# The first six weight units: VectorE sums the squares, GpSimd splits three units, and loads and products change order

## The chip, the cores and the metric

The kernel is one program on one core of a Trainium2 chip. The metric is the device time of one execution in microseconds (us). The engines are TensorE (PE, with its weight loads shown as PEld), VectorE (DVE), ScalarE (ACT), GpSimd (POOL) and the queue that issues most transfers, SyncE (SP).

## The reference

One sequence of 512 tokens, 1024 features wide, goes through two blocks. The first is RWKV-7 and mLSTM mixing with a mixture of experts, the second a convolution and a state-space mixer with a dense feed-forward. What matters here is how the first block begins:

```
mod = silu(c) @ ada_w + ada_b                 # 6 x 1024 values
sh_m, sc_m, ... = split(mod, 6)
h = x * rsqrt(mean(x * x) + EPS) * mix_norm_w * (1.0 + sc_m) + sh_m
proj = h @ w_in                               # float32, 1024 x 3336
```

## The kernel before

**Data.** Features lie on the 128 partitions, so `x` is a tile `xT` of KD = 8 pieces of 128 x 512. A weight unit is 128 x 1024 float32: eight 128 x 128 tiles that give one output tile of 128 x 512. Every float32 product is made of three passes on fp32r halves. The upper half of a weight unit is a copy with rounding (`act_upper`, on ScalarE), the lower half is the unit less that copy. The activations are split likewise: `in_h_hi` is written by ScalarE, and `dve_lower` writes the rest `h_lo` into `hT_r`. A product is upper weight x `hi`, lower weight x `hi`, upper weight x `lo`.

**The first FIRST = 6 units** have a buffer of their own (`first_w`, `first_hi_r`, `first_lo_r`) and are worked side by side by `first_units`: for each of the eight pieces k, twelve products with `hi` for the six outputs, then six with `lo`. The later units (6 and on) go through a ring of six slots, one after the other, with GpSimd making their lower halves (`pool_lower`).

**The order by engine** is written by hand, with semaphores. `S(name)` is a semaphore, and `GOES_ON` lets a name count on where another has ended.

- SP loads `c`, `x` in two halves, two modulation rows, the columns, the six units, then modulation rows 2 to 15. From row 4 on each waits until a slot of `mod_ring` (four slots) was used.
- ScalarE squares the eight pieces of `xT` into `hT`, makes the upper halves of units 0 to 2, takes the logarithm and the exponential of the sum (`act_std`: the reciprocal root), makes the upper half of unit 3, and goes into `act_shift_split`, which writes `in_h_hi` piece by piece and makes the upper halves of units 4 and 5 after piece 0.
- TensorE sums the squares over partitions with a matrix of ones (`norm_sum`: eight float32 products of two matmuls each), then does `first_units`.
- VectorE multiplies modulation rows with silu(c) and sums them (`modulate`, two rows give shift and scale of one piece), makes the gain (`early_gain`), subtracts for the lower halves (`first_lower`), and for each piece does the scaling `hT = xT * gain * rstd`, two modulation rows of a later piece, `dve_lower` and the gain. Units 3 to 5 are subtracted after piece 0's scaling, ahead of its `dve_lower`.
- GpSimd has three memsets, then waits for unit 6.

Of the kernel before, what the change touches and what calls it, by code (L numbers as in the profile page):

```python
# [11 lines left out]
ALU = mybir.AluOpType  # L12
# [69 lines left out]
for _name, _n in SMALLS:  # L82
# [134 lines left out]
    "second_arg": ("u", 8),  # L217
    "assigned": ("sa", 16),
    "totals": ("r_state_sum", 7),
    "combine": ("split_first", 6),  # L220
    "slots": ("ones", 1),
    "router_gain": ("w_t", 8),
    "router_sum": ("gn_var_done", 4),
    "moe_up": ("y_raw", 8),
# [54 lines left out]
def two_block_program(nc, x_d, w_d, mod_w_d, c_d, col_d, con_d, sma_d, lora_d, combine_d, h_d, y_d, x_kept_d, out_d):  # L279
    with ExitStack() as ctx:  # L280
        signals = {}

        def S(name):

            while name in GOES_ON:
                name = GOES_ON[name][0]
            if name not in signals:
                signals[name] = ctx.enter_context(nc.semaphore(name))
            return signals[name]

        def at_count(name, n):

            semaphore = S(name)
            while name in GOES_ON:
                name, before = GOES_ON[name]
                n = n + before
            return semaphore, n
# [2699 lines left out]
        def act_shift_split(act, name, shift, upper_r):  # L2997

            for k in range(KD):
                act.wait_ge(*at_count(name + "_scaled", k + 1))  # L3000
                act.activation(upper_r[:, k, :], hT[:, k, :], ACT.Identity, bias=mod[:, shift + k:shift + k + 1]).then_inc(S(name + "_hi"), 1)  # L3001
                if k == 0 and name == "norm_mix":
                    for u in range(4, FIRST):
                        act_upper(act, u)

        def dve_lower(dve, name, shift, upper_r, k):
# [9 lines left out]
        def act_upper(act, u):  # L3016

            if u < FIRST:
                act.wait_ge(*at_count(f"landed{u}", 16))
                act.activation(first_hi_r[:, u, :], first_w[:, u, :], ACT.Copy).then_inc(S("split_hi"), 1)  # L3020
                return
            act.wait_ge(*at_count(f"landed{u % RING}", n_landed(u)))
            if MIX_FIRST + 5 <= u < MIX_FIRST + IN_UNITS:
                act.wait_ge(*at_count("unit_done", u - 2))
            elif u > FFN_FIRST:
                act.wait_ge(*at_count("unit_done", u - 2))
            elif u >= MIX_FIRST + IN_UNITS or FIRST + 2 <= u < MIX_FIRST:
                act.wait_ge(*at_count("unit_done", u - 1))
            act.activation(hi_unit(u), ring[:, u % RING, :], ACT.Copy).then_inc(S("split_hi"), 1)  # L3029
# [51 lines left out]
        def _(pe):  # L3081
# [5 lines left out]
            def mm(out, lhsT, rhs, start=True, stop=True):  # L3087
                return pe.matmul(out, lhsT, rhs, start=start, stop=stop, skip_group_check=True)  # L3088
# [96 lines left out]
            def norm_sum(name, freed_by, by=ones):  # L3185

                out = take((name, "sum"), freed_by)
                for k in range(KD):
                    norm_add(name, out, k, by)

            def first_units():

                outs = [take(("m", u), ("m_proj", u + 1)) for u in range(FIRST)]
                for k in range(KD):
                    hi, lo = h_tiles[k]
                    w = slice(k * P, k * P + P)
                    pe.wait_ge(*at_count("norm_mix_hi", k + 1))
                    for u in range(FIRST):
                        if k == 0:
                            pe.wait_ge(*at_count("split_first", u + 1))  # L3200
                        mm(outs[u][:, :], first_hi_r[:, u, w], hi, k == 0, False)
                        mm(outs[u][:, :], first_lo_r[:, u, w], hi, False, False)
                    pe.wait_ge(*at_count("norm_mix_h", k + 1))
                    for u in range(FIRST):
                        last = mm(outs[u][:, :], first_hi_r[:, u, w], lo, False, k == KD - 1)
                        if k == KD - 1:
                            last.then_inc(S("unit_done"), 1)
                for u in range(FIRST):
                    unit[0] += 1
                    at[("unit", "m", u)] = unit[0]  # L3210

            pe.wait_ge(*at_count("ones", 1))
            norm_sum("norm_mix", ("norm_mix_std", 1), early_ones)
            h_tiles = [(in_h_hi_r[:, k, :], hT_r[:, k, :]) for k in range(KD)]

            first_units()
# [116 lines left out]
        def _(sp):  # L3333
# [29 lines left out]
            for i in range(2):  # L3363
                load_mod(i)
            sp.dma_start(col[:, :], col_d).then_inc(S("columns_landed"), 16)
            for u in range(FIRST):
                load_unit(u)
            for i in range(2, MOD_EARLY):
                load_mod(i)
            for u in range(FIRST, 2 * RING):  # L3370
                load_unit(u)
# [156 lines left out]
        def _(act):  # L3528
# [4 lines left out]
            for k in range(KD):  # L3533
                act.wait_ge(*at_count("x_landed" if k < 4 else "x_landed_b", 16))
                act_square(act, "norm_mix", k)
            for u in range(3):
                act_upper(act, u)
            act.wait_ge(*at_count("columns_landed", 16))
            act_std(act, steps, "norm_mix")
            for u in range(3, 4):  # L3540
                act_upper(act, u)
            act_shift_split(act, "norm_mix", SH_M, in_h_hi_r)
            in_units = M_TILES + R_TILES
            for u in range(FIRST, FIRST + 2):
# [101 lines left out]
        def _(dve):  # L3646
# [32 lines left out]
            def first_lower(u):  # L3679
                dve.wait_ge(*at_count("split_hi", u + 1))  # L3680
                dve.tensor_tensor(first_lo_r[:, u, :], first_w[:, u, :], first_hi_r[:, u, :].bitcast(F32), ALU.subtract).then_inc(S("split_first"), 1)

            modulate(0, 2)
            dve.wait_ge(*at_count("columns_landed", 16))
            early_gain(0)
            for u in range(3):
                first_lower(u)
            dve.wait_ge(*at_count("norm_mix_std", 1))
            for k in range(KD):
                steps.wait()  # L3690
                dve.scalar_tensor_tensor(hT[:, k, :], xT[:, k, :], gain[:, k:k + 1], rstd[:, 1, :], ALU.mult, ALU.mult).then_inc(S("norm_mix_scaled"), 1)
                if k == 0:
                    for u in range(3, FIRST):
                        first_lower(u)
                    dve_lower(dve, "norm_mix", SH_M, in_h_hi_r, k)
                    modulate(2, 4)
                    early_gain(1)
                    continue
                if k < KD - 1:
                    modulate(2 * k + 2, 2 * k + 4)  # L3700
                dve_lower(dve, "norm_mix", SH_M, in_h_hi_r, k)
                if k < KD - 1:
                    early_gain(k + 1)
# [85 lines left out]
        @block.gpsimd  # L3789
        def _(pool):  # L3790
            pool.memset(area(23680, 6 * T), 0.0)
            pool.memset(m_proj[:, :, 0:PAD], 0.0).then_inc(S("pads"), 1)
            pool.memset(early_ones, 1.0).then_inc(S("ones"), 1)
            pool_lower(pool, FIRST, M_TILES + R_TILES - FIRST, FIRST)

            def lower_out(j):
                u = OUT_FIRST + j
                pool.wait_ge(*at_count("split_hi", u + 1))
                pool.tensor_tensor(ring_r[:, u % RING, :], ring[:, u % RING, :], hi_unit(u).bitcast(F32), ALU.subtract).then_inc(S("split"), 1)

            pool_rwkv(pool, Steps(pool, S("pool_step")), lower_out)
            for j in range(KD // 2 + 1, KD):
                lower_out(j)
            pool_moe(pool)
            pool.wait_ge(*at_count("smalls_landed", 32))
            pool.tensor_tensor(dt_hi_r[:, :, :], dt_w, column("zero").rearrange("p (a b) -> p a b", a=1).broadcast_to([P, KD, 32]), ALU.add).then_inc(S("dt_hi"), 1)
            pool.wait_ge(*at_count("dt_hi", 1))
            pool.tensor_tensor(dt_lo_r[:, :, :], dt_w, dt_hi_r[:, :, :].bitcast(F32), ALU.subtract).then_inc(S("dt_lo"), 1)
            beside = pool_mix2(pool)
            for u in range(MIX_FIRST, FFN_FIRST + 3):  # L3810
                if u in TURN_UNITS:
                    continue
                at_u = u - MIX_FIRST
                if u == FFN_FIRST + 1:
                    pool.wait_ge(*at_count("norm_ffn2_added", KD - 2))
                pool.wait_ge(*at_count("split_hi", SPLIT_1 + at_u + 1))
                if u - 1 in TURN_UNITS:
                    pool.wait_ge(*at_count("split", SPLIT_1 - FIRST + at_u))
                pool.tensor_tensor(ring_r[:, u % RING, :], ring[:, u % RING, :], hi_unit(u).bitcast(F32), ALU.subtract).then_inc(S("split"), 1)  # L3819
                beside(u)  # L3820
            pool_split(pool, FFN_FIRST + 3, at["splits"] - (FFN_FIRST + 3 - MIX_FIRST), SPLIT_1 + FFN_FIRST + 3 - MIX_FIRST, 3)
# [159 lines left out]
```

## Time and profile before

| | us |
|---|---|
| median of 3 runs (1764.75 to 1767.32) | 1767.19 |
| profiled execution: time | 1761.58 |
| profiled execution: span from first to last instruction | 1759.8 |
| TensorE busy | 1664.0 (95%) |
| VectorE busy | 959.7 (55%) |
| GpSimd busy | 771.7 (44%) |
| ScalarE busy | 612.7 (35%) |
| mean granted TensorE clock | 0.985 |

Times below count from the span's start. A row of the timeline is start, duration, engine, line, instruction, operands, and how many alike instructions were merged; in brackets stand the idle time of the engine ahead of it and what ended it. A matmul of 512 columns is recorded with 0.39 us, but follows the one before at a shorter distance, since they are pipelined.

### The profile page before, as it was taken

What the parts mean: (1) busy time and instruction counts of PE and PEld (TensorE: products, weight loads), DVE (VectorE), ACT (ScalarE), POOL (GpSimd) and SP (SyncE); (2) the same over time, 40 slices, a digit from 0 to 9 for tenths busy, and PEclk for the clock granted to TensorE, in tenths of its full rate; (3) what the DMA queues carried; (4) which work ended last, traced back from release to release, by engine and by line L of the source; (5) the groups of instructions that cost most, each with busy time, mean ns of one, the idle gap of its engine ahead of it and who ended that gap; (6) DMA issues with size and microseconds to landing.
All of it is one profiled execution on the core that took longest, in us unless ns stands there. A gap on an engine that the chain in (4) does not pass through costs nothing. (4 is left out here: it accounts for less than half of the span.)

```text
span 1759.8 us, 26709 instructions
## 1 busy us (share of the span) xinstructions
PE 1664.0 (95%) x10744; PEld 1257.8 (71%) x10744; DVE 959.7 (55%) x1380; ACT 612.7 (35%) x1074; POOL 771.7 (44%) x389
## 2 busy tenths in 40 slices
PE   6999999998997888999999999899999999999998
PEld 4878678877333335778787877678887688888887
DVE  6796988654111014768888989665567422222112
ACT  4342732633322215433555544755222311111000
POOL 0442166341110112233342434534455488888884
PEclk9999999999998999999999999999999999999999
DMA  8926234456999995222122222223656233333332
GB/s 308 340 106 168 84 111 147 170 206 236 390 421 425 424 422 236 84 90 84 60 85 71 85 72 72 60 69 123 245 220 234 73 99 100 100 97 96 97 106 72
DMA packets 69127, 294.38 MB, mean 167 GB/s; under 512 B 9475, under 2 KB 9475, under 8 KB 56592
## 3 DMA queue, kind: packets, MB, share of 16 engines
q1 hardware_dynamic: 63104, 277.94, 44.0%
q0 software_dynamic: 4320, 7.93, 1.2%
q10 hardware_dynamic: 1584, 6.82, 1.0%
q8 instruction: 89, 1.46, 0.3%
q14 instruction: 30, 0.25, 0.0%
HBM read 286.56 MB, written 18.09 MB: 173 GB/s over the span
## 5 line engine op out<-in xcount | busy, mean ns | idle before, releaser
L3819 POOL TENSOR_TENSOR lo_ring<-ring,hi_ring 128x1024 fp32r<-128x1024 f32 x80 | 208.7, 2611 | 283.2 <-ACT hi_ring L3029 281.0
L3088 PE MATMUL bank<-h_lo,hi_ring 128*128 128x512 f32 x648 | 253.9, 392 | 0.0
L3088 PE MATMUL bank<-arena 64*64 64x64 f32 (+7 forms) x1736 | 196.3, 362 | 33.9 <-DMA arena<-weights_dram 26.8
L3088 PE MATMUL bank<-mix_h_hi,lo_ring 128*128 128x512 f32 x576 | 225.9, 392 | 0.0
L3088 PEld LDWEIGHTS bank<-arena 128*64 128x64 f32 (+2 forms) x1736 | 99.1, 146 | 117.7 <-issue 108.7
L3088 PE MATMUL bank<-mix_h_hi,hi_ring 128*128 128x512 f32 x416 | 165.8, 398 | 6.6 <-DVE lo_ring L2640 3.5
L2620 DVE SCALAR_TENSOR_TENSOR arena<-bank,col,arena 128x511 f32<-128x511 f32 (+14 forms) x240 | 156.5, 725 | 0.0
L3029 ACT ACTIVATE hi_ring<-ring 128x1024 fp32r<-128x1024 f32 x86 | 91.3, 1063 | 145.0 <-PE bank L3088 145.0
L3088 PEld LDWEIGHTS bank<-h_lo,hi_ring 128*128 128x128 f32 x648 | 122.4, 189 | 25.8
L3088 PE MATMUL bank<-ffn_h_hi,lo_ring 128*128 128x512 f32 x352 | 137.1, 390 | 0.0
L3088 PEld LDWEIGHTS bank<-mix_h_hi,lo_ring 128*128 128x128 f32 x576 | 109.1, 189 | 22.2 <-issue 0.5
L2922 DVE TENSOR_TENSOR arena<-arena,bank 128x512 f32<-128x512 f32 x22 | 15.2, 689 | 182.4 <-PE bank L3088 182.4
L3061 POOL TENSOR_TENSOR lo_ring<-ring,hi_ring 128x1024 fp32r<-128x1024 f32 x43 | 109.7, 2551 | 3.4
L3088 PEld LDWEIGHTS bank<-mix_h_hi,hi_ring 128*128 128x128 f32 x416 | 79.0, 190 | 26.3 <-issue 4.9
L3059 POOL TENSOR_TENSOR hi_ring<-ring,col 128x1024 fp32r<-128x1024 f32 x43 | 81.4, 1893 | 27.2 <-PE bank L3088 27.2
L2028 POOL DMA_INDIRECT y_dram<-arena,slot_table x14 | 14.1, 1006 | 176.5 <-DVE arena L1961 176.5
L3819 POOL TENSOR_TENSOR lo_ring<-ring,hi_con 128x1024 fp32r<-128x1024 f32 x16 | 40.0, 2499 | 116.5 <-ACT hi_con L3029 116.4
L3088 PE MATMUL bank<-ffn_h_hi,hi_ring 128*128 128x512 f32 x232 | 90.4, 390 | 0.0
L3664 DVE SCALAR_TENSOR_TENSOR arena<-arena,late 128x1024 f32<-128x1024 f32 x46 | 69.2, 1524 | 26.3 <-DMA arena<-mod_weights_dram 26.2
L2908 ACT ACTIVATE arena<-bank 128x512 f32<-128x512 f32 x22 | 13.2, 598 | 202.0 <-PE bank L3088 202.0
L3035 POOL TENSOR_TENSOR lo_ring<-ring,hi_ring_1a 128x1024 fp32r<-128x1024 f32 x10 | 30.7, 3068 | 110.0 <-ACT hi_ring_1a L3029 109.9
L1950 DVE TENSOR_TENSOR arena<-arena,bank 128x256 f32<-128x256 f32 x16 | 6.7, 421 | 128.6 <-ACT arena L1886 128.6
(492 smaller groups left out, 3931.2 us busy)
## 6 DMA issues: line engine op xcount, KB each, us to landing
ring<-weights_dram SPq DMA_DIRECT2D x200, 512.0 KB, 3.5
arena<-weights_dram SPq DMA_DIRECT2D x61, 1024.0 KB, 23.4
arena<-mod_weights_dram SPq DMA_DIRECT2D x54, 512.0 KB, 5.2
late<-mod_weights_dram SPq DMA_DIRECT2D x42, 512.0 KB, 4.3
ring<-weights_dram SPq DMA_DIRECT2D x15, 1024.0 KB, 25.6
hT<-weights_dram SPq DMA_DIRECT2D x10, 1024.0 KB, 27.1
late<-weights_dram SPq DMA_DIRECT2D x5, 1024.0 KB, 28.5
xT<-x_dram SPq DMA_DIRECT2D x4, 1024.0 KB, 6.0
```

Source lines behind the costliest of these rows:

```text
L1950: dve.tensor_tensor(sparse_prod, sparse_silu, bank[2 + 4 * par][:, 2 * P:4 * P], ALU.mult).then_inc(S("sparse_prod"), 1)
L2028: pool.indirect_dma_start(out=y_d, out_offset=bass.IndirectOffsetOnAxis(ap=slot_table[:, PAIRS + p:PAIRS + p + 1], axis=0), in_=y_rows[:, ...
L2620: dve.scalar_tensor_tensor(conv_y[:, k, back:T], u[:, 0:T - back], w, conv_y[:, k, back:T], ALU.mult, ALU.add).then_inc(S("conv_y"), 1)
L2908: act.activation(ffn_silu[:, n % 2, :], bank[at[("ffn_gate", n)]][:, :], ACT.Silu).then_inc(S("ffn_silu"), 1)
L2922: dve.tensor_tensor(ffn_act[:, n, :], ffn_silu[:, n % 2, :], bank[at[("ffn_up", n)]][:, :], ALU.mult).then_inc(S("ffn_act"), 1)
L3029: act.activation(hi_unit(u), ring[:, u % RING, :], ACT.Copy).then_inc(S("split_hi"), 1)
L3035: pool.tensor_tensor(ring_r[:, u % RING, :], ring[:, u % RING, :], hi_unit(u).bitcast(F32), ALU.subtract).then_inc(S("split"), 1)
L3059: pool.tensor_tensor(hi, w, column("zero").broadcast_to([P, UNIT]), ALU.add).then_inc(S("split_hi"), 1)
L3061: pool.tensor_tensor(ring_r[:, u % RING, :], w, hi.bitcast(F32), ALU.subtract).then_inc(S("split"), 1)
L3088: return pe.matmul(out, lhsT, rhs, start=start, stop=stop, skip_group_check=True)
L3664: dve.scalar_tensor_tensor(w, w, 1.0, silu_c2 if 48 <= i < MOD_OUT else silu_c, ALU.mult, ALU.mult, accum_out=mod[:, mod_column(i):mod_col ...
L3819: pool.tensor_tensor(ring_r[:, u % RING, :], ring[:, u % RING, :], hi_unit(u).bitcast(F32), ALU.subtract).then_inc(S("split"), 1)
```

## The change

It touches only the work up to the end of the first six units.

1. VectorE adds squares 1 to 6 onto square 0 (`dve_add_squares`, an existing helper), ahead of its first two modulation rows. TensorE sums two pieces, 7 and then 0, in place of eight.
2. ScalarE goes from the squares straight to logarithm and exponential, makes one upper half (unit 0), then `in_h_hi` of piece 0, then the upper halves of units 1 to 5.
3. GpSimd subtracts for the lower halves of units 1, 3 and 5 (`split_late`), VectorE for 0, 2 and 4 (`split_first`). VectorE does unit 0 and 2 around piece 0's `dve_lower`, unit 4 after the scaling of piece 1.
4. SP loads four units, two modulation rows, two units, then the other rows.
5. TensorE issues three float32 products on ones that fill the wait (`spend`), and takes the products of pieces 0 and 1 in another order; the lower halves of units 4 and 5 come in after piece 1's products with `lo`. The number of useful products is the same.

```
+    "split_first": ("norm_mix_added", 6),
+    "combine": ("split_first", 3),
+    "split_late": ("ones", 1),
+    "slots": ("split_late", 3),
 in act_shift_split
-                    for u in range(4, FIRST):
+                    for u in range(1, FIRST):
                         act_upper(act, u)
 in first_units
+                def lower(u, k):
+                    if k == 0:
+                        pe.wait_ge(*at_count("split_late" if u % 2 else "split_first", u // 2 + 1))
+                    mm(outs[u][:, :], first_lo_r[:, u, k * P:k * P + P], h_tiles[k][0], False, False)
+                def lowest(u, k):
+                    return mm(outs[u][:, :], first_hi_r[:, u, k * P:k * P + P], h_tiles[k][1], False, k == KD - 1)
+                spend(outs[0], early_ones, 3)
+                pe.wait_ge(*at_count("norm_mix_hi", 1))
+                for u in range(FIRST):
+                    pe.wait_ge(*at_count("split_hi", u + 1))
+                    mm(outs[u][:, :], first_hi_r[:, u, 0:P], h_tiles[0][0], True, False)
+                    if u == 1:
+                        lower(0, 0)
+                    if u == 2:
+                        pe.wait_ge(*at_count("norm_mix_h", 1))
+                        for v in range(3):
+                            lowest(v, 0)
+                        lower(1, 0)
+                    if u == 3:
+                        lower(2, 0)
+                        lowest(3, 0)
+                lower(3, 0)
+                lowest(4, 0)
+                lowest(5, 0)
+                for k in range(1, KD):
...
+                    pe.wait_ge(*at_count("norm_mix_hi", k + 1))
+                    if k == 1:
+                        for u in range(FIRST):
+                            mm(outs[u][:, :], first_hi_r[:, u, w], hi, False, False)
+                        for u in range(4):
+                            lower(u, k)
+                    else:
+                        for u in range(FIRST):
+                            mm(outs[u][:, :], first_hi_r[:, u, w], hi, False, False)
+                            lower(u, k)
                     pe.wait_ge(*at_count("norm_mix_h", k + 1))
                     for u in range(FIRST):
+                        last = lowest(u, k)
...
+                    if k == 1:
+                        for u in range(4, FIRST):
+                            lower(u, 0)
+                            lower(u, 1)
 TensorE ahead of first_units
-            norm_sum("norm_mix", ("norm_mix_std", 1), early_ones)
+            out = take(("norm_mix", "sum"), ("norm_mix_std", 1))
+            pe.wait_ge(*at_count("norm_mix_square", KD))
+            mm(out[:, :], early_ones, hT[:, KD - 1, :], True, False)
+            pe.wait_ge(*at_count("norm_mix_added", KD - 2))
+            mm(out[:, :], early_ones, hT[:, 0, :], False, True).then_inc(S("norm_mix_sum"), 1)
 SyncE
-            for u in range(FIRST):
+            for u in range(4):
                 load_unit(u)
-            for i in range(2, MOD_EARLY):
+            for i in range(2, 4):
+                load_mod(i)
+            for u in range(4, FIRST):
+                load_unit(u)
+            for i in range(4, MOD_EARLY):
                 load_mod(i)
 ScalarE
-            for u in range(3):
-                act_upper(act, u)
             act.wait_ge(*at_count("columns_landed", 16))
             act_std(act, steps, "norm_mix")
-            for u in range(3, 4):
-                act_upper(act, u)
+            act_upper(act, 0)
 VectorE
+            for k in range(1, KD - 1):
+                dve_add_squares(dve, "norm_mix", k)
             modulate(0, 2)
             dve.wait_ge(*at_count("columns_landed", 16))
             early_gain(0)
-            for u in range(3):
-                first_lower(u)
             dve.wait_ge(*at_count("norm_mix_std", 1))
...
                 if k == 0:
-                    for u in range(3, FIRST):
-                        first_lower(u)
+                    first_lower(0)
                     dve_lower(dve, "norm_mix", SH_M, in_h_hi_r, k)
+                    first_lower(2)
                     modulate(2, 4)
                     early_gain(1)
+                    continue
+                if k == 1:
+                    first_lower(4)
+                    dve_lower(dve, "norm_mix", SH_M, in_h_hi_r, k)
+                    modulate(4, 6)
+                    early_gain(2)
                     continue
 GpSimd, ahead of pool_lower
+            for u in range(1, FIRST, 2):
+                pool.wait_ge(*at_count("split_hi", u + 1))
+                pool.tensor_tensor(first_lo_r[:, u, :], first_w[:, u, :], first_hi_r[:, u, :].bitcast(F32), ALU.subtract).then_inc(S("split_late"), 1)
```

## Rows read from the trace of the kernel before

**Rows 1.** Stretches: us, busy PE, PEld, DVE, ACT, POOL, clock, DMA, GB/s
```profile
22.67:26.10 3.43, 3.43 (x10) 2.65 (x9) 3.43 (x4) 0.77 (x1) 0.00 (x0) 0.52 0.81 331
...
30.00:58.00 28.00, 28.00 (x124) 23.16 (x125) 26.03 (x52) 6.58 (x9) 3.13 (x2) 1.00 0.91 321
58.00:97.00 39.00, 39.00 (x174) 30.39 (x173) 29.81 (x29) 13.38 (x19) 19.84 (x10) 1.00 0.87 325
```

**Rows 2.** Waits from 13 to 60 us: in total, times, longest
```profile
ACT in_h_hi L3001 <- DVE hT L3691: 25.3, 7, 5.6
```

**Rows 3.** Timeline of TensorE
```profile
8.93 8.79 PE L3088 MATMUL bank<-hT,arena 128*128 128x512 f32 x16 [8.93 <-ACT hT L2953]
...
29.82 0.50 PE L3088 MATMUL bank<-in_h_hi,first_hi 128*128 128x512 f32 x1 [2.24 <-ACT in_h_hi L3001]
...
34.04 0.39 PE L3088 MATMUL bank<-in_h_hi,first_hi 128*128 128x512 f32 x1
...
58.55 0.39 PE L3088 MATMUL bank<-in_h_hi,hi_ring_1a 128*128 128x512 f32 x1
```

**Rows 4.** The sum's matmuls, in ns: shortest, median, longest
```profile
L3088 PE MATMUL bank<-hT,arena x16: 592/593/1190, 8.9 to 17.1; 128*128 128x512 f32 x16
```

**Rows 5.** Timeline of ScalarE
```profile
8.16 2.19 ACT L2953 ACTIVATE hT<-xT 128x512 f32<-128x512 f32 x4 [0.34 <-DMA xT<-x_dram]
10.61 2.19 ACT L2953 ACTIVATE hT<-xT 128x512 f32<-128x512 f32 x4 [0.27 <-DMA xT<-x_dram]
15.18 1.06 ACT L3020 ACTIVATE first_hi<-arena 128x1024 fp32r<-128x1024 f32 x1 [2.38 <-DMA arena<-weights_dram]
...
18.66 0.67 ACT L2969 ACTIVATE rstd<-bank,col 128x512 f32<-128x512 f32 x1
...
21.45 1.99 ACT L3020 ACTIVATE first_hi<-arena 128x1024 fp32r<-128x1024 f32 x2
```

**Rows 6.** Timeline of VectorE, pieces 0 to 2
```profile
20.02 0.75 DVE L3691 SCALAR_TENSOR_TENSOR hT<-xT,gain,rstd 128x512 f32<-128x512 f32 x1
...
22.53 2.36 DVE L3681 TENSOR_TENSOR first_lo<-arena,first_hi 128x1024 fp32r<-128x1024 f32 x2 [0.34 <-ACT first_hi L3020]
24.80 0.75 DVE L3009 SCALAR_TENSOR_TENSOR h_lo<-hT,mod,in_h_hi 128x512 fp32r<-128x512 f32 x1
25.46 1.22 DVE L3664 SCALAR_TENSOR_TENSOR arena<-arena,late 128x1024 f32<-128x1024 f32 x1
...
28.26 0.75 DVE L3691 SCALAR_TENSOR_TENSOR hT<-xT,gain,rstd 128x512 f32<-128x512 f32 x1
...
32.27 0.75 DVE L3691 SCALAR_TENSOR_TENSOR hT<-xT,gain,rstd 128x512 f32<-128x512 f32 x1
```

**Rows 7.** GpSimd's first subtraction, with nothing of size beside them on VectorE
```profile
54.87 2.41 POOL L3035 TENSOR_TENSOR lo_ring<-ring,hi_ring_1a 128x1024 fp32r<-128x1024 f32 x1 [51.12 <-ACT hi_ring_1a L3029]
```

**Rows 8.** Places where GpSimd and VectorE meet, from three stretches of the timeline
```profile
65.39 2.48 POOL L3035 TENSOR_TENSOR lo_ring<-ring,hi_ring_1a 128x1024 fp32r<-128x1024 f32 x1 [5.76 <-ACT hi_ring_1a L3029]
...
65.65 3.31 DVE L3664 SCALAR_TENSOR_TENSOR arena<-arena,late 128x1024 f32<-128x1024 f32 x1
...
888.50 1.60 POOL L2537 TENSOR_TENSOR arena<-arena 128x512 f32<-128x512 f32 x1 [4.08 <-ACT arena L2344]
888.86 1.78 DVE L2632 SCALAR_TENSOR_TENSOR late<-arena,col,late 128x512 f32<-128x512 f32 x1
...
1382.72 4.65 POOL L3819 TENSOR_TENSOR lo_ring<-ring,hi_ring 128x1024 fp32r<-128x1024 f32 x2 [2.03 <-DVE hT L2959]
...
1386.17 2.41 DVE L2990 SCALAR_TENSOR_TENSOR hT<-xT,gain,rstd 128x512 f32<-128x512 f32 x2 [3.45 <-ACT rstd L2971]
```

**Rows 9.** GpSimd behind a chain of VectorE's
```profile
100.53 8.03 DVE L628 SCALAR_TENSOR_TENSOR arena<-arena,col 128x512 f32<-128x512 f32 x12
103.64 7.15 POOL L3035 TENSOR_TENSOR lo_ring<-ring,hi_ring_1a 128x1024 fp32r<-128x1024 f32 x1 [8.46 <-ACT hi_ring_1a L3029]
```

**Rows 10.** An addition of squares without GpSimd beside it
```profile
1381.96 0.68 DVE L2959 TENSOR_TENSOR hT<-hT 128x512 f32<-128x512 f32 x1
```

More of the change, by code:

```diff
@@ L219 @@
     "totals": ("r_state_sum", 7),
-    "combine": ("split_first", 6),
-    "slots": ("ones", 1),
+    "split_first": ("norm_mix_added", 6),
+    "combine": ("split_first", 3),
+    "split_late": ("ones", 1),
+    "slots": ("split_late", 3),
     "router_gain": ("w_t", 8),
@@ L3193, in first_units @@
                 outs = [take(("m", u), ("m_proj", u + 1)) for u in range(FIRST)]
-                for k in range(KD):
+                def lower(u, k):
[23 more added lines that the diff above has]
+                for k in range(1, KD):
                     hi, lo = h_tiles[k]
@@ L3197, in first_units @@
                     pe.wait_ge(*at_count("norm_mix_hi", k + 1))
-                    for u in range(FIRST):
[L3199 to L3202, printed above, removed]
+                    if k == 1:
[7 more added lines that the diff above has]
+                            lower(u, k)
                     pe.wait_ge(*at_count("norm_mix_h", k + 1))
                     for u in range(FIRST):
-                        last = mm(outs[u][:, :], first_hi_r[:, u, w], lo, False, k == KD - 1)
+                        last = lowest(u, k)
                         if k == KD - 1:
                             last.then_inc(S("unit_done"), 1)
+                    if k == 1:
+                        for u in range(4, FIRST):
+                            lower(u, 0)
+                            lower(u, 1)
                 for u in range(FIRST):
@@ L3365, in _ @@
             sp.dma_start(col[:, :], col_d).then_inc(S("columns_landed"), 16)
-            for u in range(FIRST):
+            for u in range(4):
                 load_unit(u)
-            for i in range(2, MOD_EARLY):
+            for i in range(2, 4):
[3 more added lines that the diff above has]
+            for i in range(4, MOD_EARLY):
                 load_mod(i)
```

## The prediction

> **What bounds the kernel now.** I read the table of stretches first, since the change ends with the sixth unit. From 30 to 58 us TensorE has no idle time, and none from 58 to 97 us [rows 1]. So whatever the start gains or loses moves the whole of what follows, as long as TensorE stays the last to be ready there. Ahead of that TensorE does wait. TensorE's first product of piece 1 ended a wait of 2.24 us for `in_h_hi` [rows 3], and ScalarE, which writes it, waited 25.3 us for VectorE's scaling over the seven later pieces [rows 2]. So the chain is VectorE's scaling, ScalarE's `in_h_hi`, TensorE. From the start of the scaling of piece 1 (28.26) to TensorE's first product on it (29.82) it is 1.56 us [rows 3, 6].
>
> From then on two periods run side by side. TensorE needs 18 products a piece, and goes from 29.82 over 34.04 to 58.55: the six pieces from the second of these take 24.51 us, 4.08 us each, which is 0.227 us a product [rows 3]. VectorE goes from scaling to scaling in 32.27 - 28.26 = 4.01 us [rows 6]. These nearly tie. Whoever brings TensorE to piece 2 earlier or later sets the end of the first units, since VectorE has only 0.07 us in hand for each later piece to catch up. I therefore work out when VectorE starts the scaling of piece 2: 32.27 now.
>
> **The sum of squares.** Now it ends at 17.72 (8.93 + 8.79) [rows 3], and the logarithm starts at 18.66, because ScalarE was still at the third upper half. From the logarithm to the scaling of piece 0 it is 20.02 - 18.66 = 1.36 us [rows 5, 6]. After the change the last square is done at 10.61 + 2.19 = 12.80 [rows 5]. VectorE's six additions cost 0.68 us each [rows 10], say 0.72 with the wait for the one before; the first can start when the second square is done (8.16 + 1.1 [rows 5]), so they end at about 13.6. They are hidden behind the product of piece 7. VectorE's two modulation rows and the gain come after them, at about 13.6 + 2.9 = 16.5, when VectorE would else be idle. TensorE has four matmuls left. The slowest of the sixteen now take 1190 ns against 593 ns for most [rows 4]; the four at the start were at half pace, one each 0.86 us. A TensorE that has done nothing starts at half pace, so I take four at 0.86 from 12.85: 16.3, and about 0.2 to the end of the last. The scaling of piece 0 then starts at 16.5 + 1.4 = 17.9, against 20.02: 2.1 us gained. At full pace it would be 14.8, but then the gain (16.5) is last, so 16.5 is the bound on the other side.
>
> **VectorE from there, without GpSimd.** The pitches, start to start, are: scaling 0.67, `first_lower` (24.80 - 22.53) / 2 = 1.14, `dve_lower` 25.46 - 24.80 = 0.66, two modulation rows and a gain 28.26 - 25.46 = 2.80 [rows 6]. ScalarE makes the upper half of unit 0 first (1.0 us, to 18.9), then `in_h_hi` (to 19.6), then unit 1 (to 20.5), unit 2 (to 21.5), unit 3 (to 22.5); units 4 and 5 come behind two more transfers of their size. Now unit 0 is there at 15.18 and unit 5 by 22.4 [rows 5], at most 1.45 us each, so they are there at some 24 and 25 (an estimate), and unit 5's upper half at 25 to 26. VectorE: scaling 17.9, `first_lower(0)` 18.95 to 20.1, `dve_lower` to 20.75, then a wait for unit 2's upper half to 21.5, `first_lower(2)` to 22.65, rows and gain to 25.45: scaling of piece 1 there, 2.8 us ahead of 28.26. Then `first_lower(4)`, `dve_lower`, rows and gain: 0.67 + 1.14 + 0.66 + 2.80 = 5.27, so the scaling of piece 2 at 30.7, 1.55 us ahead of 32.27. Unit 4's upper half is needed by VectorE only at 26.1. Its subtraction is no longer between pieces 0 and 1, but it is still ahead of piece 2. The loads cost nothing: modulation rows 2 and 3 land where units 4 and 5 did, by 22.4, and are read from 22.65 on.
>
> **What GpSimd's three subtractions cost.** One takes 2.4 us of GpSimd [rows 7], against 1.14 us on VectorE. More important is what they do to VectorE. At 65.65 a modulation row that takes 1.22 us elsewhere took 3.31 us. GpSimd's subtraction had got in at about 65.5, in the gap between two rows (the read of the accumulator, 0.08 us), and ended at 67.87; VectorE's ended 1.09 us later. The same shows at 888.86 for a `scalar_tensor_tensor` of 512 columns that reads two tiles: 1.78 us, where the scaling, of like size, has 0.75. For the very operation of this stage, the scaling at 1386.17, two took 2.41 us where one takes 0.75, behind two GpSimd subtractions that end at 1387.37 [rows 8]. So an instruction of VectorE that reads two tiles of SBUF waits for GpSimd's whole subtraction. All of VectorE's in this stage read two tiles. GpSimd for its part is passed over while VectorE's follow each other without a gap: 7.15 us at 103.64 [rows 9].
>
> The Trainium skill ("SBUF — State Buffer", section "Who interferes with whom") states this as one rule: VectorE with two SBUF inputs and a GpSimd instruction that reads SBUF need the same port pair, and whoever issues first holds it to its end. The rows at 65.65 and 1386.17 agree. By first-come alone GpSimd would be served ahead of the two modulation rows, by the row at 103.64 perhaps only after one or both; where each subtraction falls differs, the time of piece 2's scaling does not.
>
> Put into the chain. Unit 1's subtraction gets in at 20.75, while VectorE waits anyway until 21.5, and ends at 23.15: `first_lower(2)` is 1.65 us later. Unit 3's is ready by then; at 888.50 the two engines took turns [rows 8], so VectorE goes first with `first_lower(2)` and perhaps one modulation row, and GpSimd then takes 2.4 us. Unit 5's (upper half at 25.0) follows at the next gap, 2.4 us more. Sum: 1.65 + 2.4 + 2.4 = 6.45 us. The scaling of piece 1 comes at 25.45 + 6.45 = 31.9 (now 28.26), that of piece 2 at 30.7 + 6.45 = 37.15, against 32.27: 4.9 us later. If unit 5's falls behind the scaling of piece 1, piece 1 is 2.4 us earlier and piece 2 the same.
>
> **TensorE.** Piece 0's products are spread over the upper halves and end with those of unit 3's lower half at some 28.8; TensorE then waits until 31.9 + 1.56 = 33.5 (now 29.82). Its 20 products in piece 1 last 4.5 us, to 38.0, and piece 2 can start at 37.15 + 1.56 = 38.7, against 34.04 now: 4.7 us later. That it starts on time holds only at full clock. From 22.67 to 26.10 us the granted clock was 0.52, the half level of 1.2 GHz in place of 2.4, soon after the idle time that began at 17.72 [rows 1, 3]. If the same falls on piece 1, its products take up to 1.6 us more, end at 39.6, and piece 2 is 0.9 us later still. The three products of `spend` end at about 19 at full pace (21.5 at half) and delay at most piece 0, which has slack until 33.5. So 4.7 to 5.6 us for the end of the first units; I take 5.0. The ring's units 6 and 7, split at 55 to 60 now, are moved by the same 5 us and stay 1 us ahead of TensorE, because their upper halves come behind piece 7's `in_h_hi`.
>
> The profiled execution took 1761.58 us around a span of 1759.8, and is 5.6 us under the median of 1767.19. The change of 5.0 us is added to either: 1766.6 for an execution like the profiled one, 1772.2 for the median. A difference under 0.2% (3.5 us) can't be told from none for this kernel.
>
> **The rivals.**
> - *The delay is taken up later.* Against it: no idle time of TensorE up to 97 us [rows 1]. For it: VectorE and ScalarE do idle behind the first units, and later stages wait on transfers, which a shift could meet otherwise. Then 1 to 3 us are left: about 1769.5.
> - *No collision.* Were the subtractions to run beside VectorE, only the gains stand: piece 2 at 30.7 + 1.56 = 32.3 against 34.04, 1.7 us faster: 1765.5, not slower, and inside the 0.2%. This decides if the three cost VectorE less than about 1.5 us together (then the chain breaks even), and rows 8 speak against it in each kind of instruction.
> - *The clock falls and stays low longer, or GpSimd's last subtraction holds back unit 5 in piece 1.* TensorE then is late in piece 2 as well: 6 to 8 us, about 1774.
> - *The squares' sum gains nothing.* If additions and cold matmuls end no earlier than 17.7, piece 0 starts 1.2 us later than I have it, and the total is about 1773.2. This stands inside the range.
>
> **How the numbers follow.** The forecast, with the subtractions blocking VectorE and the shift carried to the end, 1772.2, has 0.64 (with the last rival in it); the delay partly taken up 0.15; no collision 0.12; the longer low clock 0.07; something outside the list that makes it over 0.2% faster 0.02. The range from 1766.0 to 1774.5 covers the forecast's own 1770.9 to 1773.6, most of the partial case and a part of the others. Slower by over 0.2%, that is over 1770.7: 0.52 of the 0.64 (the rest of it is lost to the spread of the runs), nearly all of the 0.07, 0.02 of the partial case: 0.60. Within 0.2%: 0.37. Faster: 0.03.
>
> **What would show it.** Right: the scaling of piece 0 near 18, piece 1 near 32, piece 2 near 37; three subtractions on GpSimd from about 20.8, VectorE instructions of 2.8 to 3.6 us among them; TensorE's first ring product near 63.5. Wrong: VectorE's instructions at 0.7 to 1.2 us beside GpSimd's, or the first ring product before 59.

## The result and the profile after

The changed kernel took 1770.47 us against 1766.57 us (medians of 19 runs each, 3.9 us apart). The ratio over all the runs is 1.0025 with a 95% interval of 1.0014 to 1.0036: 4.4 us slower, between 2.5 and 6.4. Run again beside other kernels it was 1.0020 (1.0006 to 1.0034), 3.5 us. The forecast was 5.0 us slower. That the kernel is slower is clear of the noise in both; that it is slower by over 0.2%, to which the prediction gave 0.60, is not settled, since 1.0020 lies inside both intervals.

The first 64 us show why. First VectorE in the changed kernel, against [rows 6]; the columns are those of the timeline:

```profile
17.96 0.75 DVE L3733 SCALAR_TENSOR_TENSOR hT<-xT,gain,rstd 128x512 f32<-128x512 f32 x1 [1.29 <-ACT rstd L2973]
...
21.41 2.71 DVE L3723 TENSOR_TENSOR first_lo<-arena,first_hi 128x1024 fp32r<-128x1024 f32 x1 [0.62 <-ACT first_hi L3022]
24.05 3.39 DVE L3706 SCALAR_TENSOR_TENSOR arena<-arena,late 128x1024 f32<-128x1024 f32 x1
...
27.37 3.35 DVE L3706 SCALAR_TENSOR_TENSOR arena<-arena,late 128x1024 f32<-128x1024 f32 x1
...
31.15 0.75 DVE L3733 SCALAR_TENSOR_TENSOR hT<-xT,gain,rstd 128x512 f32<-128x512 f32 x1
...
36.41 0.75 DVE L3733 SCALAR_TENSOR_TENSOR hT<-xT,gain,rstd 128x512 f32<-128x512 f32 x1
```

Piece 0 is scaled 2.06 us earlier than before (17.96 for 20.02), piece 1 2.89 us later (31.15 for 28.26), piece 2 4.14 us later (36.41 for 32.27). Between them stand three VectorE instructions that are too long. GpSimd beside them, all three subtractions in one row and then the last alone:

```profile
20.52 9.12 POOL L3844 TENSOR_TENSOR first_lo<-arena,first_hi 128x1024 fp32r<-128x1024 f32 x3 [16.76 <-ACT first_hi L3022]
...
26.31 3.32 POOL L3844 TENSOR_TENSOR first_lo<-arena,first_hi 128x1024 fp32r<-128x1024 f32 x1
```

GpSimd's are 2.4 us of work each [rows 7]. Each of them falls on one VectorE instruction, which takes 2.71, 3.39 and 3.35 us where it has 1.22 elsewhere: 1.49 + 2.17 + 2.13 = 5.79 us. TensorE pays for it, against [rows 3]:

```profile
12.85 3.63 PE L3090 MATMUL bank<-hT,arena 128*128 128x512 f32 x4 [12.85 <-ACT hT L2955]
...
32.71 2.93 PE L3090 MATMUL bank<-in_h_hi,first_hi 128*128 128x512 f32 x6 [5.33 <-ACT in_h_hi L3003]
...
39.25 0.39 PE L3090 MATMUL bank<-in_h_hi,first_hi 128*128 128x512 f32 x1
...
63.73 0.39 PE L3090 MATMUL bank<-in_h_hi,hi_ring_1a 128*128 128x512 f32 x1
```

It waited 5.33 us for piece 1. Its first product of piece 2 stands at 39.25 in place of 34.04, and its first product on a ring unit stands at 63.73 in place of 58.55. I use this last number below as the measure of the first units, "the first ring product", since the time of a whole run spreads by some 10 us. The clock, in the table of stretches with the columns of [rows 1]:

```profile
29.50:33.00 3.50, 0.29 (x1) 0.29 (x2) 3.39 (x7) 0.72 (x1) 0.13 (x1) 0.55 0.55 177
33.00:36.00 3.00, 3.00 (x8) 2.32 (x8) 2.99 (x6) 0.00 (x0) 0.00 (x0) 0.50 0.20 79
```

Piece 1's products ran at the half level (0.50, 1.2 GHz) up to 36 us and a little beyond (0.91 is the mean from 36 to 40). Behind 63.73 TensorE is busy without a break to 102 us, as it was before to 97.

### The profile page after: what moved, and what is told of

Its sections match the earlier page's. It is cut to its first block and busy times, and to the rows that moved or that the text cites. A ratio compares the mean times of both kernels' runs of the same rounds, so it can differ in the third digit from the quotient of the medians.

```text
span 1772.8 us, 26708 instructions
## 1 busy us (share of the span) xinstructions
PE 1666.3 (94%) x10738; PEld 1257.5 (71%) x10738; DVE 966.3 (55%) x1383; ACT 613.5 (35%) x1074; POOL 781.0 (44%) x392
## 5 line engine op out<-in xcount | busy, mean ns | idle before, releaser
L3090 PEld LDWEIGHTS bank<-ffn_h_hi,lo_ring 128*128 128x128 f32 x352 | 66.1, 188 | 13.5
## 6 DMA issues: line engine op xcount, KB each, us to landing
arena<-weights_dram SPq DMA_DIRECT2D x61, 1024.0 KB, 24.5
```

## The experiments

**All six on VectorE** (`e1_all_vector`). The change, less its use of GpSimd:

```
...
-                    first_lower(2)
+                    for u in range(1, 4):
+                        first_lower(u)
 at k == 1
+                    first_lower(5)
 GpSimd
-            for u in range(1, FIRST, 2):
-                ...
```

> The change, but VectorE subtracts all six units (1 to 3 after piece 0's dve_lower, 4 and 5 after piece 1's scaling) and GpSimd none. Theory, GpSimd's subtractions block VectorE: three subtractions of 1.14 us on VectorE replace the blocking; scaling of piece 1 at about 26.9 us, of piece 2 at 33.3, first ring product near 59.4 us (63.73 in the changed kernel, 58.55 before), so time within 1.5 us of before. Rival, the order of loads and products costs the time: piece 2 later than 35 and the first ring product at 62 or later, time 3 to 5 us over before.

```profile
20.68 3.49 DVE L3723 TENSOR_TENSOR first_lo<-arena,first_hi 128x1024 fp32r<-128x1024 f32 x3
...
26.89 0.75 DVE L3733 SCALAR_TENSOR_TENSOR hT<-xT,gain,rstd 128x512 f32<-128x512 f32 x1
...
33.29 0.75 DVE L3733 SCALAR_TENSOR_TENSOR hT<-xT,gain,rstd 128x512 f32<-128x512 f32 x1
```

Three subtractions take 3.49 us on VectorE, and piece 2 comes at 33.29, as worked out (33.3): 3.12 us earlier than with GpSimd, though VectorE does three more. The first ring product is at 60.12, 0.7 us later than expected, because TensorE again ran at half clock (0.50 from 29.5 to 33 us). The ratio is 0.9991 (0.9975 to 1.0008): the loss is gone. A second execution (`all_vector_b`, below) had the full clock there (1.00), waited 1.57 us for piece 2 and had the first ring product at 59.52. So in this kernel the half clock in piece 1 cost 0.6 us, and VectorE sets the rest.

**Writing in place of subtracting** (`e2_memset`). GpSimd is kept as busy, but reads nothing; the lower halves of units 1, 3 and 5 are left out:

```
             for u in range(1, FIRST, 2):
+                pool.wait_ge(*at_count("split_late", u // 2))
                 pool.wait_ge(*at_count("split_hi", u + 1))
-                pool.tensor_tensor(first_lo_r[:, u, :], ...)
+                pool.memset(area(23680, 6 * T), 0.0).then_inc(S("split_late"), 1)
 in lower(u, k)
-                    mm(outs[u][:, :], first_lo_r[:, u, ...], ...)
+                    mm(outs[u][:, :], (first_hi_r if u % 2 else first_lo_r)[:, u, ...], ...)
```

> The change, but in place of its three subtractions GpSimd writes zeros over an area nobody uses then (128 x 3072, some 2.7 us each, reads nothing), and TensorE takes the upper halves of units 1, 3 and 5 in place of the lower: the lower halves of three units are left out, with as many products. Theory, VectorE waits for GpSimd's reading: VectorE's instructions are 0.7 to 1.2 us beside the writes, scaling of piece 1 near 25.5 us, of piece 2 near 30.8, first ring product between 56.8 and 57.7 us. Rival, any GpSimd instruction of this length or the semaphores between the engines delay VectorE: piece 2 near 36 and first ring product near 63.

GpSimd and VectorE in this run:

```profile
20.66 8.14 POOL L3845 MEMSET arena<- 128x3072 f32 x3 [16.91 <-ACT first_hi L3022]
```
```profile
22.66 1.22 DVE L3706 SCALAR_TENSOR_TENSOR arena<-arena,late 128x1024 f32<-128x1024 f32 x1
...
30.73 0.75 DVE L3733 SCALAR_TENSOR_TENSOR hT<-xT,gain,rstd 128x512 f32<-128x512 f32 x1
```

GpSimd was busy for 8.14 us and VectorE's rows beside it have their 1.22 us. Piece 2 is at 30.73 and the first ring product at 56.95, both as worked out for the case without collision; the ratio is 0.9983 (0.9969 to 0.9998). The semaphores and the hand-over to GpSimd are the same but for one wait more on GpSimd, so they are not what costs: it is something in the subtraction itself. A memset differs from it in two ways, it reads nothing and it computes nothing. The trace of the kernel before tells these apart. There the same subtraction of GpSimd's meets VectorE instructions of two kinds, one that takes a tile from a PSUM bank and one from SBUF, and one that takes both from SBUF:

```profile
819.48 2.41 POOL L3819 TENSOR_TENSOR lo_ring<-ring,hi_ring 128x1024 fp32r<-128x1024 f32 x1 [3.46 <-ACT hi_ring L3029]
819.92 0.68 DVE L2659 TENSOR_TENSOR arena<-bank,arena 128x512 f32<-128x512 f32 x1
...
851.34 2.40 POOL L3819 TENSOR_TENSOR lo_ring<-ring,hi_ring 128x1024 fp32r<-128x1024 f32 x1 [4.06 <-ACT hi_ring L3029]
851.42 2.73 DVE L2695 TENSOR_TENSOR arena<-arena,rstd 128x384 f32<-128x384 f32 x1
```

The first kind (lines 2652 and 2659) starts inside a GpSimd subtraction in twelve places of that trace and has its 0.68 us in each; the second (line 2695) does so in twelve too, and has 1.98 to 2.74 us in place of 0.56. So what costs is that GpSimd reads SBUF while VectorE reads two tiles from it. By the Trainium skill ("SBUF — State Buffer", section "Who interferes with whom") a VectorE instruction with two SBUF inputs contends with a GpSimd instruction that reads SBUF, and not with one that only writes it; the changed kernel and this run agree, one with each half.

**Only GpSimd's part, in the kernel before** (`e3_only_pool`):

```
...
             for u in (0, 2):          # before the scaling, was range(3)
                 first_lower(u)
...
-                    for u in range(3, FIRST):
-                        first_lower(u)
+                    first_lower(4)
 GpSimd
+            for u in range(1, FIRST, 2): ...tensor_tensor(...)
```

> The kernel before with one part of the change: GpSimd subtracts units 1, 3 and 5, VectorE 0, 2 and 4; everything else in the old order. Theory, each subtraction blocks VectorE for up to 2.4 us where it falls on its work: scaling of piece 0 near 21.0 us (20.02 before), of piece 2 near 35.0 (32.27), first ring product near 61.3 us, time 2 to 3 us over before. Rival, taking two units off VectorE between pieces 0 and 1 helps: piece 2 ahead of 32, first ring product at 58.5 or earlier.

```profile
24.73 2.85 DVE L3010 SCALAR_TENSOR_TENSOR h_lo<-hT,mod,in_h_hi 128x512 fp32r<-128x512 f32 x1
...
34.30 0.75 DVE L3692 SCALAR_TENSOR_TENSOR hT<-xT,gain,rstd 128x512 f32<-128x512 f32 x1
```

Piece 0 was scaled at 20.75 and piece 2 at 34.30, 0.7 and 2.0 us later than before, and the first ring product came at 60.55: the sign was as expected, the size 0.7 us smaller. The `dve_lower` at 24.73 took 2.85 us in place of 0.75. Taking work off VectorE made VectorE later. The 2 to 3 us that I expected in the run's time did not show: the ratio can't be told from none (0.9998, 0.9982 to 1.0014).

**TensorE kept busy between pieces 0 and 1** (`e4_warm`). The change, with `spend(bank[7], early_ones, 6)` after piece 0's last product.

> The change, with six further float32 products on ones into an unused bank between piece 0 and piece 1, in TensorE's wait from 27.3 to 32.7 us. Theory, piece 1 ran at the half clock because TensorE had idled: its twenty products take 4.5 us in place of 6.5, piece 2 starts at 38.0 us in place of 39.25, first ring product near 62.5 us, time 1.2 us under the changed kernel. Rival, VectorE alone sets it or the clock stays low: first ring product at 63.5 or later.

```profile
29.50:33.00 3.50, 3.33 (x9) 1.36 (x8) 3.40 (x7) 0.72 (x1) 0.00 (x0) 1.00 0.53 172
```

The clock stayed at 1.00 through piece 1, TensorE waited 0.47 us for piece 2, and the first ring product, at 62.48, came 1.25 us earlier than in the change's first profile. So of the 5.2 us between the two first profiles, some 1.3 are the clock's and 3.9 VectorE's. The ratio of 1.0011 (0.9995 to 1.0028) lies under the change's, not clear of it.

**The best order without GpSimd** (`e5_early_warm`). `e1_all_vector`, with unit 0's upper half ahead of the logarithm, its subtraction ahead of the scaling, unit 1's upper half ahead of `in_h_hi`, and two products on ones between the pieces:

```
...
+            act_upper(act, 0)
             act_std(act, steps, "norm_mix")
-            act_upper(act, 0)
+            act_upper(act, 1)
 VectorE
             early_gain(0)
+            first_lower(0)
             dve.wait_ge(*at_count("norm_mix_std", 1))
...
```

> The change without GpSimd's subtractions (VectorE does all six), with unit 0's upper half made ahead of the logarithm and subtracted ahead of the scaling of piece 0 (both in idle time), unit 1's upper half made ahead of piece 0's in_h_hi, and two float32 products on ones between pieces 0 and 1. Theory: scaling of piece 0 at 17.9 us, piece 1 at 25.8, piece 2 at 32.2, TensorE at full pace in piece 1, first ring product near 58.3 us, so time within 0.5 us of before and some 5 us under the changed kernel. Rival, the first units' order costs by itself: first ring product over 59.5.

Pieces 0, 1 and 2 at 17.80, 25.62 and 32.03, first ring product at 58.22. It undoes the loss, and shows how little there is to gain: VectorE's work up to piece 2 fills its time, and the first units end 0.3 us ahead of the first profile of before and level with its third. The ratio is 0.9999 (0.9986 to 1.0012), against the change's 1.0020 beside it.

**The sum over eight pieces** (`e6_eight`). The change with the old sum: `norm_sum(...)` on TensorE in place of the two products, and no `dve_add_squares`.

> The change with the sum of squares as before: TensorE sums eight pieces, VectorE adds none; the logarithm still comes ahead of the upper halves. Theory, half of the 2.1 us at piece 0 is the removed upper half ahead of the logarithm and the other half the shorter sum: scaling of piece 0 near 19.1 us, of piece 2 near 37.6, first ring product at 64 to 65 us. Rival, VectorE's additions give nothing: scaling of piece 0 at 18.0.

The scaling of piece 0 is at 19.17, of piece 2 at 37.63, 1.2 us later than in the change. Of the 2.06 us gained at piece 0, 1.2 are the shorter sum's and the rest (0.85) the upper half that no longer stands ahead of the logarithm. The first ring product, at 65.78, was 0.8 us over the range; TensorE was at the half clock in piece 1 again (0.50 from 33 to 36 us, 0.53 from 36 to 40). This is the prediction's rival that the sum gains nothing: it would have added 1.2 us. A single execution (1768.02 us) says nothing of the run's time.

**Repeats.** The changed kernel, the kernel before and the all-VectorE kernel once more:

> The changed kernel once more, beside the others on one chip. Theory: the first 64 us repeat to within 0.3 us (piece 2 at 36.4, first ring product near 63.7 or, with the full clock in piece 1, 62.5), while the wait for a modulation row near 175 us (9.9 us in the first profile, 5.2 in the kernel before) varies from execution to execution. Rival: the change itself causes that later wait; then it is near 9.9 us again. Time over before by 2 to 6 us.

> The kernel before once more, unchanged, to see whether VectorE's wait for a modulation row near 175 us (5.2 us in its first profile, 9.0 to 9.9 in two profiles of the changed kernel) belongs to the execution or to the kernel. If to the execution, before can show 9 us as well; if to the kernel, it shows 5 us in each profile. The first units repeat: first ring product at 58.3 to 58.8 us.

> The changed kernel a third time. If the wait near 175 us belongs to the execution, it is now either near 5 or near 9 us; if to the kernel, near 9 again. First ring product at 63.2 to 63.8 us either way.

> As before_b: the kernel before, a third profile. Wait near 175 us of 5 in each if it belongs to the kernel, of 5 or 9 if to the execution.

> The kernel of e1_all_vector once more (8.9 us of wait in its first profile, whose time was 8 us over the median of its runs). If the wait belongs to the execution, it can be near 5 us here, and the time then is near the median, 1762 us. First ring product at 59.4 to 60.2 us.

| profile | first ring product, us | wait for a row near 175 us | that execution, us |
|---|---|---|---|
| before, three profiles | 58.55, 60.09, 58.22 | 5.16, 3.81, 3.13 | 1761.58, 1761.05, 1758.20 |
| changed, three profiles | 63.73, 63.28, 64.29 | 9.87, 9.02, 3.51 | 1774.52, 1775.12, 1768.00 |
| all on VectorE, two | 60.12, 59.52 | 8.87, 3.77 | 1770.90, 1760.42 |
| `e5_early_warm` | 58.22 | 9.17 | 1764.07 |
| `e4_warm`, `e3_only_pool`, `e2_memset` | 62.48, 60.55, 56.95 | 4.90, 4.60, 2.86 | 1765.37, 1760.21, 1757.07 |

The means of three are 58.95 and 63.77: the change costs the first units 4.8 us, in reach of both ratios (4.4 and 3.5 us). Both kernels vary by 1 to 2 us there, and most of it is TensorE's clock in piece 1: VectorE's scaling of piece 2 varies by 0.3 us only (31.97 to 32.27 before, 36.33 to 36.52 changed), and its means are 4.3 us apart. In the profile of before with 60.09 TensorE had the half clock from 31.3 to 34 us (0.50), which my expectation of 58.3 to 58.8 had left out. `after_again` came 0.45 us from the first profile where I had expected 0.3, and `after_c` was over its range by 0.5.

## Why the prediction was right, step by step

- **What bounds the kernel** held. The scaling of piece 2 moved by 4.14 us and the first ring product by 5.2 in the first profiles; the ratio gives 4.4 us for the whole time, the medians themselves 3.9.
- **The sum of squares.** 17.9 forecast, 17.96 measured. TensorE's four matmuls took 0.86 us each from start to start (12.85 to 16.31), as I had taken, twice the 0.43 of the six on ones behind them. The profile gives a granted clock of 1.00 for that stretch, so that this is the half clock is not shown. VectorE's additions and rows were hidden (the gain was ready at 16.7). `e6_eight` splits the gain.
- **Without GpSimd.** Piece 1 at 25.45 and piece 2 at 30.7 forecast; `e2_memset` gave 25.46 and 30.73.
- **The price of the collisions** was the term that was sized too high: 1.65 + 2.4 + 2.4 = 6.45 forecast, 1.49 + 2.17 + 2.13 = 5.79 measured. A blocked VectorE instruction is longer by less than GpSimd's 2.4 us; the row at 65.65 [rows 8] said so already, with 3.31 - 1.22 = 2.09 us, and I took the whole length. So piece 2 was at 36.41 and not at 37.15.
- **The clock** was the term that was sized too low. I gave it up to 1.6 us in piece 1 against 0.7 us in hand ahead of piece 2 (38.0 to 38.7), so up to 0.9 us, and took a third of that, 0.3. In the first profile the time in hand was the same 0.7 us: at full pace piece 1 would have ended at 32.71 + 4.54 = 37.25, and VectorE had piece 2 ready at 36.41 + 1.56 = 37.97. But piece 1's products took 6.54 us (32.71 to 39.25), 2.0 more than 4.54, so TensorE was 1.28 us late; `e4_warm` gave back 1.25. In the two repeats TensorE was late by 0.9 and 1.7 us (first product of piece 2 at 38.80 and 39.81).
- **The two errors nearly cancel**, and that is luck. Collisions and what goes with them were 0.7 us too dear (3.9 in place of 4.7 for VectorE's part), the clock 1.0 us too cheap (1.3 in place of 0.3). So 5.0 was forecast and 5.2 came, and piece 2's first product was at 39.25, within my 38.7 to 39.6.
- **Turns.** I let GpSimd in after the first modulation row; it got in ahead of it, at the switch from `first_lower(2)` to the row. As forecast, the place made no difference to piece 2.
- **The rivals.** "No collision" is out (`e1_all_vector` and `e2_memset` against the change). "Taken up later" can't be excluded for a part: over the six timed kernels the time moved by 2.5 us less to 0.5 us more than the first ring product did, less in five of the six, each inside its own interval. "The squares' sum gains nothing" is out by `e6_eight`; added up as the prediction has it, it would give 1772.2 + 1.2 = 1773.4, not 1773.2. That a mere order of loads and products costs is out too: `e2_memset` has that order and gains.

## What to carry to other kernels

Before work is moved from VectorE to GpSimd, look at what both read: if VectorE's instructions beside it take two tiles from SBUF, most of GpSimd's time is added to VectorE's, and a subtraction of 1.14 us on VectorE was replaced by about 1.9 us of standing still. Move it only to where VectorE idles or takes one of its two tiles from PSUM, or give GpSimd work that only writes. And a chain with a period of 4.01 us beside one of 4.08 makes up next to nothing: what is lost ahead of piece 2 is still lost behind piece 7. From TensorE's first product of piece 2 to its first ring product it was 24.5 to 24.7 us in all thirteen profiles.

## What the runs showed of the hardware that was not expected

The modulation row that VectorE waits for near 175 us, in a part of the kernel that the change doesn't touch, came early or late: the wait was 2.9 to 5.2 us in nine profiles and 8.9 to 9.9 us in four, in the changed and in the all-VectorE kernel with both values. The executions with the long wait were 6.5 to 10.5 us longer than the short ones of the same kernel, in the two kernels that showed both; the one of `e5_early_warm`, at 1764.07 us, does not stand out among its twelve runs (1759.84 to 1767.90).

Ahead of the row on the queue stands a 4 MB transfer that clears `y_dram`. VectorE read the row 24.9 to 27.2 us after that clear was issued, in all thirteen profiles, whether the row was issued 7.3 us behind the clear (the four long waits) or 11.0 to 11.3 us (the nine others). So the row comes late when the clear is issued late. The clear was issued 88.2 to 88.7 us after the first ring product in the nine, and 91.7 to 93.4 us in the four. It stands behind a load that waits until VectorE has read an earlier modulation row.

Up to 145 us the change's first profile and `after_c` run level, VectorE to 0.05 us. Then, first the one with the long wait, then the one with the short:

```profile
144.94 2.89 POOL L3037 TENSOR_TENSOR lo_ring<-ring,hi_ring_1a 128x1024 fp32r<-128x1024 f32 x1 [13.22 <-ACT hi_ring_1a L3031]
145.61 2.77 DVE L1216 SCALAR_TENSOR_TENSOR arena<-arena,col 128x512 f32<-128x512 f32 x1
```
```profile
145.66 0.75 DVE L1216 SCALAR_TENSOR_TENSOR arena<-arena,col 128x512 f32<-128x512 f32 x1
```

It is the same collision. In `after_c` the subtraction starts at 146.62 and finds this instruction done. The next subtraction, at 152.18, falls on the modulation row itself (2.70 us in place of 1.23). Both VectorE instructions have the long time in all four profiles with the long wait (2.77 us; 2.47 to 2.70) and the short one in all nine others (0.75; 1.22 or 1.23). The subtraction comes early because ScalarE's upper half does (at 143.81 in place of 145.49), and that is released by TensorE; what lies behind this was not followed. That the collision decides the long wait fits all thirteen profiles, but no run forced it. Whether the kernel before can have it is open: its three profiles did not show it. If the change brings it about more often, a part of the 4.4 us comes from here and not from the first units.
